# 16x16 diagonal blocks of the triangular inverses: substitution on VectorE in place of doubling on TensorE

## The reference, cut to what matters

```python
def step(S, inp):
    r_t, w_t, k_t, v_t, a_t, b_t = inp
    sa = jnp.einsum('bhvk,bhk->bhv', S, a_t)
    S = S * w_t[:, :, None, :] + sa[..., :, None] * b_t[..., None, :] + v_t[..., :, None] * k_t[..., None, :]
    y = jnp.einsum('bhvk,bhk->bhv', S, r_t)
    return S, y
```

## Time and profile before

| | us |
|---|---|
| median of 3 runs (lowest, highest) | 3540.36 (3539.9, 3541.68) |
| profiled execution, first to last instruction | 3531.5 |
| PE busy in it | 3408.7 |
| DVE busy in it | 1523.3 |
| rounds 2 to 9, in the profiled execution | about 133 to 570 |

### The profile page before, as it was taken

How to read it: one execution, slowest core, us unless ns; L and a number is a source line. 1 busy time by engine, 2 the same in 40 slices (tenths; PEclk the granted TensorE clock), 3 DMA queues, 4 the chain that set the end, 5 groups by cost and what they waited for, 6 DMA issues and landing times.

```text
span 3531.5 us, 56015 instructions
## 1 busy us (share of the span) xinstructions
PE 3408.7 (97%) x24870; PEld 2234.4 (63%) x24870; DVE 1523.3 (43%) x2761; ACT 755.8 (21%) x1572; POOL 353.7 (10%) x274
## 2 busy tenths in 40 slices
PE   7999998999999999999999899999999999899999
PEld 3566676888884658788886456656445656534344
DVE  4454454788743225678732445444212204201011
ACT  2333332211003025211002223223222320211111
POOL 0010110232001000122100111003000001100000
PEclk9999999999999999999999999999999999899999
DMA  5321202255651320156522110100111114599997
GB/s 197 120 73 46 86 7 85 87 176 179 203 155 49 84 72 1 49 171 192 173 73 80 41 37 25 37 25 2 57 60 48 48 37 155 233 422 421 421 422 283
DMA packets 355810, 453.12 MB, mean 128 GB/s; under 512 B 25713, under 2 KB 282993, under 8 KB 331761
## 3 DMA queue, kind: packets, MB, share of 16 engines
q1 hardware_dynamic: 355568, 449.55, 37.0%
HBM read 445.27 MB, written 4.20 MB: 127 GB/s over the span
## 4 chain that ended last, share of the span: by engine, by line
PE 89%; DVE 5%; DMA 3%; ACT 2%; issue 1%; SPq 0%; POOLq 0%; POOL 0%; DVEq 0%; ACTq 0%
PE bank L79 88%; DMA A<-in_w_up 2%; DVE A L70 1%; DVE A L76 1%; ACT A L87 1%; DMA W<-in_w_up 1%; PE bank L82 0%; DVE H L70 0%; ACT SM L87 0%; DVE X L76 0%; DVE A L73 0%; DVE SM L76 0%; DMA A<-in_x 0%; ACT H L87 0%; ACT L90 0%
## 5 line engine op out<-in xcount | busy, mean ns | idle before, releaser
L79 PE MATMUL bank<-A 64*64 64x64 f32 (+4 forms) x13728 | 1069.6, 261 | 45.7 <-ACT A L87 25.4
L79 PEld LDWEIGHTS bank<-A 64*64 64x64 f32 (+2 forms) x13728 | 855.1, 148 | 306.2 <-issue 139.5
L79 PE MATMUL bank<-A,W 128*128 128x256 f32 (+1 forms) x2240 | 719.3, 475 | 2.6 <-DMA W<-in_rw_g 1.4
L79 PE MATMUL bank<-H,W 128*128 128x512 f32 (+2 forms) x1712 | 637.0, 522 | 18.5 <-ACT H L87 14.4
L79 PEld LDWEIGHTS bank<-A,W 128*128 128x128 f32 x2240 | 417.8, 191 | 253.5 <-issue 213.0
L87 ACT ACTIVATE A<-bank 128x512 f32<-128x512 f32 (+5 forms) x517 | 222.8, 435 | 1498.1 <-PE bank L79 1454.5
L79 PEld LDWEIGHTS bank<-H,W 128*128 128x128 f32 (+1 forms) x1712 | 313.1, 190 | 275.0 <-issue 244.3
L79 PE MATMUL bank<-A,H 128*64 128x512 f32 (+2 forms) x1224 | 309.6, 573 | 6.4 <-DMA A<-in_w_up 3.5
L70 DVE TENSOR_TENSOR A<-bank,A 128x256 f32<-128x256 f32 (+1 forms) x350 | 157.7, 462 | 182.7 <-PE bank L79 161.5
L79 PEld LDWEIGHTS bank<-A,H 128*64 128x64 f32 (+1 forms) x1224 | 114.0, 145 | 171.8 <-issue 150.7
L70 POOL TENSOR_TENSOR A<-A 128x512 f32<-128x512 f32 (+1 forms) x103 | 145.7, 1421 | 732.8 <-ACT A L87 372.7
(11 more groups left out here) (179 smaller groups left out, 2509.9 us busy)
## 6 DMA issues: line engine op xcount, KB each, us to landing
A<-in_w_gate SPq DMA_DIRECT2D x47, 1024.0 KB, 22.7
W<-in_mod_w SPq DMA_DIRECT2D x45, 1024.0 KB, 7.2
A<-in_w_up SPq DMA_DIRECT2D x42, 1024.0 KB, 19.3
A<-in_w_down SPq DMA_DIRECT2D x35, 1024.0 KB, 27.0
W<-in_mlp_up SPq DMA_DIRECT2D x64, 512.0 KB, 5.4
W<-in_mlp_down SPq DMA_DIRECT2D x128, 256.0 KB, 4.0
W<-in_w_mod SPq DMA_DIRECT2D x24, 1024.0 KB, 5.3
W<-in_w_up SPq DMA_DIRECT2D x22, 1024.0 KB, 19.0
```

Of the source, the lines that this page charges most:

```text
L79: return self.e.matmul(o, l, r, start=start, stop=stop, skip_group_check=True)
```

## The change

Levels 0 to 3 of the doubling are left out: the sets u0, u1, t1, tt1, u2, t2, tt2, u3, t3, tt3 of TensorE, with VectorE's t0, a1, a2, a3, tt1, tt2, tt3, ScalarE's three copies of t and GpSimd's tt0. u4, t4, tt4, u5, tt5 stay in their slots.

In their place VectorE turns M by 32x32 blocks (`e.transpose`, 128x512) so that each of the pair's 64 diagonal 16x16 blocks (8 chunks, 2 heads, 4 blocks) lies in one partition as 256 elements, in `XI` (the other 64 partitions hold nothing of use). Two masked operations pick the right half (new constant columns 68 and 69 of "iota", `parity`), a memset puts ones on the diagonal, and 14 steps of substitution follow, each of two dependent tensor_tensor operations on (15-j) x j elements: 14 elements for j = 1, 56 for j = 7 and 8, 14 for j = 14. ScalarE and GpSimd then spread XI out again (two operations of 128x256 each, masked by `parity`), and two more 32x32 turns on VectorE give `T_` and `TT` as level 4 wants them. `XI` lies in the memory of T_, the blocks before and after in that of A_.

```diff
+    for n in range(2):
+        f[:, 68 + n] = np.arange(128) % 4 == np.arange(128) % 64 // 32 * 2 + n
...
+        def by16(v):
+            return v.rearrange("p s (b c) -> p c s b", b=4)
+        def of16(v):
+            return v.rearrange("p (c j) -> p c j", j=32)
+        def parity(n, rows=slice(0, P)):
+            return C("iota")[rows, 68 + n:69 + n]
+        def solve16(dv, x, tmp, j):
+            n = 15 - j
+            t = tmp[:, 0:n * j].rearrange("p (i c) -> p i c", i=n)
+            dv.wait_ge(s_dv, ndv.n)
+            dv.tt(t, x[:, j + 1:16, j:j + 1].broadcast_to([P, n, j]), x[:, j:j + 1, 0:j].broadcast_to([P, n, j]), MUL).then_inc(s_dv, ndv())
+            dv.wait_ge(s_dv, ndv.n)
+            return dv.tt(x[:, j + 1:16, 0:j], x[:, j + 1:16, 0:j], t, ADD)
...
+        XI, XTMP = TM[:, 0:256].rearrange("p (i c) -> p i c", i=16), TM[:, 256:320]
... pe_scores
-            pe.wait_ge(s_gp, ngp["m", ct])
-            for c in range(8):
-                for h in half:
-                    m = pe.mm(bank8(4)[h, c, :], m8[h, c, :], rcon("r64", rows=h), True, True)
-            m.then_inc(s_pe, npe("u", ct, 0))
...
-                if lev == 1:
-                    pe.wait_ge(s_dv, ndv["t", ct, 0])
-                    each(x, m8, T_).then_inc(s_pe, npe("u", ct, lev))
-                yield
-                if lev == 1:
-                    pe.wait_ge(s_gp, ngp["tt0", ct])
-                else:
+                yield
+                if lev > 3:
                     pe.wait_ge(s_dv, ndv["tt", ct, lev - 1])
-                pe.wait_ge(s_dv, ndv["a", ct, lev])
-                if lev < 5:
+                    pe.wait_ge(s_dv, ndv["a", ct, lev])
+                if lev == 4:
                     each(y, TT, A_).then_inc(s_pe, npe("t", ct, lev))
-                each(x, A_, TT).then_inc(s_pe, npe("tt", ct, lev))
+                if lev > 3:
+                    each(x, A_, TT).then_inc(s_pe, npe("tt", ct, lev))
...
-                if lev < 5:
-                    pe.wait_ge(s_ac, nac["t", ct, lev])
+                if lev == 3:
+                    pe.wait_ge(s_gp, ngp["m", ct])
+                    pe.wait_ge(s_dv, ndv["t", ct, 3])
+                elif lev == 4:
+                    pe.wait_ge(s_ac, nac["t", ct, 4])
+                if lev in (3, 4):
                     each(y, m8, T_).then_inc(s_pe, npe("u", ct, lev + 1))
... gp_scores
-            gp.wait_ge(s_dv, ndv["sb", ct, 1])
+            gp.wait_ge(s_dv, ndv["raw", ct])
             gp.tt(m8, m8, over8("r64", 0), ADD).then_inc(s_gp, ngp("m", ct))
-            gp.tt(TTs[ct % 2], m8, over8("r64", 64), MUL).then_inc(s_gp, ngp("tt0", ct))
...
+            yield from idle(4)
+            gp.wait_ge(s_dv, ndv["inv", ct])
+            for n in range(2):
+                gp.ts(of16(AM)[:, :, 16 * n:16 * n + 16], XI, parity(n), None, MUL, None).then_inc(s_gp, ngp() if n == 0 else ngp("ett", ct))
... ac_scores, in s11
+                if lev == 3:
+                    ac.wait_ge(s_dv, ndv["inv", ct])
+                    for n in range(2):
+                        m = ac.act(of16(TTf)[:, :, 16 * n:16 * n + 16], XI.rearrange("p i c -> p c i"), COPY, scale=parity(n))
+                        m.then_inc(s_ac, nac() if n == 0 else nac("et", ct))
... dv_scores, in s1 behind the masks
+            dv.wait_ge(s_dv, ndv.n)
+            dv.e.transpose(of16(AM), by16(NRs[ct % 2][:, :, 0, :])).then_inc(s_dv, ndv("raw", ct))
+            yield
+            dv.wait_ge(s_dv, ndv.n)
+            dv.ts(XI, of16(AM)[:, :, 0:16], parity(0), None, MUL, None).then_inc(s_dv, ndv())
+            dv.wait_ge(s_dv, ndv.n)
+            dv.stt(XI, of16(AM)[:, :, 16:32], parity(1), XI, MUL, ADD).then_inc(s_dv, ndv())
+            dv.wait_ge(s_dv, ndv.n)
+            dv.e.memset(TM[:, 0:256:17], 1.0).then_inc(s_dv, ndv())
+            for j in range(1, 15):
+                if j in (2, 3, 4, 6, 7, 9, 11, 13):
+                    yield
+                if j == 2:
+                    masked("sk", AKs[ct % 2], 2, 0)
+                if j == 6:
+                    masked("sk", AKs[ct % 2], 2, 1)
+                solve16(dv, XI, XTMP, j).then_inc(s_dv, ndv() if j < 14 else ndv("inv", ct))
+            yield
+            yield
+            dv.wait_ge(s_ac, nac["et", ct])
+            dv.wait_ge(s_gp, ngp["ett", ct])
+            dv.e.transpose(by16(T_), of16(TT.rearrange("p c t -> p (c t)"))).then_inc(s_dv, ndv("t", ct, 3))
+            dv.wait_ge(s_dv, ndv.n)
+            dv.e.transpose(by16(TT), of16(AM)).then_inc(s_dv, ndv("tt", ct, 3))
```

More of the change, by code:

```diff
@@ L743, in program @@
         TTs = [c8(cv(512)) for _ in range(2)]
-        T_, A_ = c8(cv(512)), c8(cv(512))
+        TM, AM = cv(512), cv(512)
+        T_, A_ = c8(TM), c8(AM)
+        XI, XTMP = TM[:, 0:256].rearrange("p (i c) -> p i c", i=16), TM[:, 256:320]
         Yb, t2 = cv(512), cv(512)
@@ L1037, in gp_scores @@
             yield from idle(2)
-            gp.wait_ge(s_dv, ndv["sb", ct, 1])
+            gp.wait_ge(s_dv, ndv["raw", ct])
             gp.tt(m8, m8, over8("r64", 0), ADD).then_inc(s_gp, ngp("m", ct))
-            gp.wait_ge(s_gp, ngp.n)
-            if ct >= 2:
-                gp.wait_ge(s_pe, npe["headed", ct - 2])
-            gp.tt(TTs[ct % 2], m8, over8("r64", 64), MUL).then_inc(s_gp, ngp("tt0", ct))
             yield from idle(3)
@@ L1049, in gp_scores @@
                 yield
-            yield from idle(17)
+            yield from idle(4)
+            gp.wait_ge(s_dv, ndv["inv", ct])
+            for n in range(2):
+                gp.ts(of16(AM)[:, :, 16 * n:16 * n + 16], XI, parity(n), None, MUL, None).then_inc(s_gp, ngp() if n == 0 else ngp("ett", ct))
+            yield from idle(13)
         def ac_scores(ac, ct):
+            TTf = TTs[ct % 2].rearrange("p c t -> p (c t)")
             yield from idle(5)
@@ L1083, in dv_scores @@
             masked("sb", NRs[ct % 2], 5, 1)
+            dv.wait_ge(s_dv, ndv.n)
[15 more added lines that the diff above has]
+                solve16(dv, XI, XTMP, j).then_inc(s_dv, ndv() if j < 14 else ndv("inv", ct))
             yield
             yield
-            masked("sk", AKs[ct % 2], 2, 0)
+            dv.wait_ge(s_ac, nac["et", ct])
[3 more added lines that the diff above has]
+            dv.e.transpose(by16(TT), of16(AM)).then_inc(s_dv, ndv("tt", ct, 3))
             yield
-            dv.wait_ge(s_pe, npe["u", ct, 0])
-            dv.tt(T_, bank8(4), over8("r_lev0", 0), MUL).then_inc(s_dv, ndv("t", ct, 0))
             yield
-            masked("sk", AKs[ct % 2], 2, 1)
-            for lev in range(1, 6):
+            for lev in range(4, 6):
                 x = 5 if lev % 2 else 4
                 dv.wait_ge(s_pe, npe["u", ct, lev])
-                if lev > 1:
+                if lev == 4:
+                    dv.wait_ge(s_dv, ndv["tt", ct, 3])
+                else:
                     dv.wait_ge(s_pe, npe["tt", ct, lev - 1])
-                dv.tt(A_, bank8(x), over8(f"r_lev{lev // 2 * 2}", 64 * (lev % 2)), MUL).then_inc(s_dv, ndv("a", ct, lev))
+                dv.tt(A_, bank8(x), over8("r_lev4", 64 * (lev % 2)), MUL).then_inc(s_dv, ndv("a", ct, lev))
                 yield
```

## The result

Side by side on one chip, in three rounds, the changed kernel takes 3549.15 us (median, 13 runs) and the kernel before 3542.05 (13 runs): a ratio of 1.0016, interval [1.0009, 1.0024] (the two medians by themselves are 7.1 us apart, 1.0020). On the scale of the 3540.36 us of before that is 5.7 us slower, with 3491 predicted (49.6 us faster). The profiled execution has a span of 3547.4 us.

A forecast was written before the change was run, and what follows sets the result against it. TensorE bounds rounds 2 to 7: 58.2 us saved, less 7.6 load, 5.1 clock, 2.0 round 2, 3.0 bank 2, plus 2.8 and 8.0 in rounds 8 and 9, less 1.7 clock: 49.6 us faster, 3491 us (range 3474 to 3512).

The forecast's parts named there:

- The path to u4: From inv through GpSimd's spreads and the turn into T_: ready before TensorE reaches u4 in rounds 4 to 7.
- the load's stops: In s12, TensorE waits for rw_g ahead of g, 1.9 us in each of rounds 4 to 7: 7.6 us.
- 7.6 + 2.0 + 3.0: Charges for rw_g's load, for TensorE waiting on VectorE and GpSimd in round 2, and for bank 2 handoffs.
- The clock: Half-level stretches behind three of four load stops, 5.1 us; one more in rounds 8 and 9, 1.7 us.
- The worth of the sets: Ten sets off TensorE: 9.7 us a round, 58.2 us in rounds 2 to 7, at most 19.4 in 8 and 9.
- Bank 2 and VectorE in rounds 3 to 7: VectorE and TensorE meet at bank 2 with nothing in hand, 0.5 us a round, 3 us; VectorE doesn't bind overall.
- The price of the 32x32 turn: Each 128x512 turn on VectorE takes 0.7 us, range 0.54 to 1.9; three turns a round, 2.1 us.
- Rounds 8 and 9: Rounds without a fetch: VectorE sets the pace from s0 to s10 in round 8; gains 2.8 and 8.0 us.
- VectorE lags in s1 to s10: Rival: dearer turns or steps held back by GpSimd make VectorE late, 4 us a round: 3502 to 3530 us; 18%.
- Slower: Rival: short substitution steps cost about 1.5 us each, so VectorE bounds all rounds: +97, 3637 us; 4%.
- Two of its own signs: Signs of being wrong: a turn above 1 us; TensorE waiting for VectorE over 1 us a round in 3 to 7.
- The 8.9 us: Median lies 8.9 us above the profiled span, for what lies around it; kept when turning span 3481.9 into 3491.

The follow-up runs named there:

- later g: Changed kernel with TensorE's product g of post two slots later (s14), behind the landing of its load; 3542.18 us, ratio 1.0003 to the kernel before.
- spreads first: Changed kernel with GpSimd's two spreads one slot earlier, ahead of BH's product; 3509.28 us, ratio 0.9908 to the kernel before.
- both placements: Changed kernel with GpSimd's spreads one slot earlier and TensorE's g two slots later; 3495.89 us, ratio 0.9870 to the kernel before.
- filler sets: Changed kernel plus unread constant sets on TensorE, four ahead of u4 and two in s12; 3546.7 us, ratio 1.0018 to the kernel before.
- no steps: Changed kernel without the 28 short substitution operations on VectorE, inverses not computed; 3539.84 us, ratio 0.9993 to the kernel before.
- both, no steps: Kernel with both placements, without the 28 short substitution operations, inverses not computed; 3487.85 us, ratio 0.9849 to the kernel before.
- spreads first, ten sets back: Kernel with the spreads first, plus ten unread constant sets on TensorE in the slots they were taken from; 3539.63 us, ratio 0.9998 to before.
- both, first turn later: Kernel with both placements, with VectorE's 32x32 turn of the raw blocks one slot later; ratio 0.9892 to the kernel before.
- before, late load: Kernel before, with load rw_g issued only after tt3 in rounds 4 to 7; ratio 1.0053 to the kernel before.
- spreads on ScalarE: Changed kernel with g two slots later and all four spreads on ScalarE, none on GpSimd; 3497.49 us, ratio 0.9878 to the kernel before.

## Why the prediction was wrong

**The step that failed** is "The path to u4: inv at 25.7, kkn 26.4; GpSimd first does BH behind kkn (1.7), then two spreads", which ended in "not late". It gave BH's product one input, kkn. The product has another wait, which stands ahead of that one in `gp_prep`:
```
gp.wait_ge(s_pe, npe["tok", ct - 1, 2])     # the turn of the old BH, s13
gp.wait_ge(s_dv, ndv["kkn", ct])
```
Before, nobody needed GpSimd between s10 and the end of the round, and VectorE's bh, which needs it, comes after s13 anyway: VectorE itself waits for the same turn an operation earlier, at kh. So the time that GpSimd stands there, 27.40 us in round 7 of before, left no row among TensorE's waits:
```profile
475.48 1.77 POOL L70 TENSOR_TENSOR X<-X 128x512 f32<-128x512 f32 x1 [27.40 <-PE bank L79]
```
The change put u4's input behind this wait, and so behind TensorE's own s13. The runs price the step: 38 us when only the queue is changed (1.0016 to 0.9908), and beside the later g 47 us when the queue is changed (1.0003 to 0.9870) and 44 when the work leaves GpSimd (to 0.9878). In place of "not late" u4 was 4.35 us late in each of seven rounds, 30.4 us; what the 38 have above that is clock.

**What is left without that step.** The kernel that the prediction described, with the load's stops and without u4's, is the one with the spreads first: 32.6 us faster than before, 3508 on the scale of before, where 49.6 and 3491 were predicted. It is inside the stated range, near its slow end, and 17 us off. The kernel with both placements is at 3494, 3 us from the predicted time, but this is luck: it lacks the stops of the load, for which the prediction charged 7.6 us and 5.1 of clock. The 17 us are taken apart next.

The table goes from 90 us to the first copy of round 10's chain in the profiled execution of each kernel, in us against before. "Copy" is how much later it comes, "idle" the idle time of TensorE, "clock" half of the time that it worked at half level, and "the rest" what is then left: TensorE's work at full clock. Single executions differ by some us.

| kernel | copy | idle | clock | the rest |
|---|---|---|---|---|
| after | +9.8 | +53.0 | +22.6 | -65.8 |
| spreads first | -29.8 | +22.9 | +13.5 | -66.3 |
| g later | +3.5 | +48.2 | +24.6 | -69.3 |
| filler sets | +6.0 | +20.9 | +6.4 | -21.3 |
| no steps | +1.0 | +46.2 | +18.4 | -63.6 |
| both placements | -44.0 | +18.5 | +5.1 | -67.5 |
| both, no steps | -56.3 | +14.1 | -4.5 | -65.9 |
| spreads first, ten sets back | +3.2 | +1.5 | -2.8 | +4.5 |
| both, first turn later | -40.4 | +21.3 | +7.4 | -69.0 |
| before, late load | +15.6 | +8.6 | +5.1 | +1.9 |
| spreads on ScalarE | -43.9 | +20.4 | 0.0 | -64.3 |

For the kernel with the spreads first the prediction had, in these terms, 21.2 of idle time (7.6 + 2.0 + 3.0, and 8.6 for the part of the sets that rounds 8 and 9 don't give), 6.8 of clock, and 77.6 for the sets. Measured are 22.9, 13.5 and 66.3. So the idle time was right in sum, the clock was 7 us too low and the worth of the sets 11 too high.

**The load**: forecast four stops of 1.9, measured 7.1 in all. Right, by the cover that went: 1.75 us ahead of g in round 7.

**The clock.** Behind the load's stops it was right: in the kernel with the spreads first three of the four are followed by half level, for 3.4, 6.8 and 3.4 us, which costs 6.8 us where 5.1 were charged. The other 7 us lie elsewhere, in part behind stops of 1 to 2.2 us in rounds 8 and 9, in part behind none. The thinner stream as such costs little clock: with the sets still out, the four kernels without u4's and the load's stops are at +5.1, -4.5, +7.4 and 0.0. The prediction weighed the Trainium skill here (TensorE: Matmul & The Clock Gate, section Why this matters for your kernels), which warns of long idle gaps; by it the stops of about 2 us would have been worth their length alone, 8 us in the kernel with the late load, and the measured 18.8 (13 to 24) speaks for the row and against it, as was argued.

**The worth of the sets, and ScalarE's handoffs**, which had no term. The chain's uu and ds wait for copies that a set used to cover: 43 to 65 times, 14.3 to 21.7 us, and 25.8 with both placements. The sets put back bring it to 14.3 again. The same handoffs seem to be in "the rest" too: the other 64x64 records on `A`, some 2980 in either kernel, are busy 110.3 us with the spreads first and 105.7 with the ten sets back (half level counted half). That is 4.6 of the 11 us; where the others lie the runs don't tell.

**Bank 2 and VectorE in rounds 3 to 7**: 3 us were charged; over all rounds the waits for X rose from 1.3 to 3.5 us, of which 0.9 lie in rounds 3 to 7. VectorE doesn't bind there, as claimed: without its steps the five rounds are 4.0 us shorter. The price of the 32x32 turn was wrong, 1.04 us for 0.7. The estimate from the page in the prediction (the Trainium skill, VectorE: DVE Perf Modes, section The three transpose paths) was also worked out wrongly: four times 311 ns is 1.24 us, not 0.7.

**Rounds 8 and 9**: forecast a gain of 2.8 + 8.0. From first copy to first copy before takes 41.8 and 36.5 us (499.12 to 540.95 to 577.43); with the spreads first 40.9 and 32.5, a gain of 4.9; with both placements 42.4 and 34.8, a gain of 1.1; without the steps 39.2 and 30.6, a gain of 8.5. The prediction had VectorE set the pace from s0 to s10 with 20.3 us, against the 20.8 that the stretch takes before, so nothing was in hand for what it had not priced. The turn at 1.04 in place of 0.7 adds 0.3 there, and the step beside GpSimd's pair 1.5, where 1.0 was charged.

**The rivals.** "VectorE lags in s1 to s10" named steps held back beside GpSimd. Such a step is there (1.88 us), and leaving all steps out is worth 7 us, mostly in rounds 8 and 9; what the holding back costs by itself wasn't tested. "Slower" was to come from dear steps; slower it is, through another engine's queue, on which no rival stood. Its size, 1.0016, is under the 0.2% that the prediction called "same" and gave 1%. The range ended at 3512 because no case priced GpSimd's order. Two of its own signs came: a turn costs more than 1 us, and TensorE waits more than 1 us a round for VectorE in rounds 3 to 7, by the turn into `T_`.

**The 8.9 us** between the profiled span and the median were put down to what lies around the program. Only 1.8 of them are: every profiled run of the other kernels took 1.8 us more than its span. So the profiled execution of before was one of about 3533 us, 7.1 faster than the median. It makes no difference to the 3491, but the differences in the table are against a fast execution.

**Open.** Behind round 10's copy no stage is changed, yet the clock over the next 43 us differs, before first, then both placements:
```profile
577.00:620.00 43.00, 35.14 (x306) 24.08 (x307) 21.45 (x39) 9.06 (x24) 0.00 (x0) 0.88 0.34 91
533.00:576.00 43.00, 36.25 (x277) 23.01 (x278) 16.26 (x29) 9.06 (x24) 0.00 (x0) 0.64 0.23 60
```
That is 10 us more of lost clock in one execution, and whether the change or chance brings it no run tells. Nor why one stop of 2.2 us is followed by half level and another isn't: of the 20.5 us that before spends at half level from 90 us to the copy, only 3.4 follow a stop of over 0.9 us.

## What to carry to other kernels

When work is handed to an engine that was idle, look not at its busy time but at what each instruction already in its queue waits for: GpSimd was 10% busy, and its queue still stood for 23.5 us of round 7, by waits that hurt nobody until something was queued behind them. Ask of the engine that is relieved what its removed work covered, copies and loads alike, and count a stop dearer than its length, since the clock often follows. When a gain is missing, first add up idle time and half level up to the same piece of work in both kernels: that told here where 75.6 us had gone. And when one step of a forecast fails, compare the forecast with the kernel that lacks only that fault, not with the one that comes nearest to it.

## What was not expected of the hardware

- A 32x32 turn of 128x512 float32 on VectorE takes 1.04 us, 1.5 times a copy of that size (0.69).
- Two VectorE operations of 128x36 take 1.88 us beside two of GpSimd, 0.43 alone; GpSimd's pair takes 2.04, and VectorE ends as it ends, like the scans of the earlier trace rows.
- Added stops of 8.0 us in a full stream cost 18.8 us (13 to 24).
- A GpSimd tensor_scalar of 128x256 takes 0.93 us, ScalarE's of the same data 0.73.
